# The w3 pieces of the experts issued by GpSimd from a queue of its own

## The chip, the cores and the metric

The kernel runs on one core of a Trainium2 chip. The time is device microseconds of one execution: 1745.23 us, the median of three runs (1743.76 to 1749.59).

## What is computed

Two layers of a backbone over 256 context and 256 latent tokens of width 1024. Each layer mixes tokens and then channels. The channel mixer of the second layer, on the latent tokens alone, is a mixture of 8 SwiGLU experts with hidden width 3584, two chosen for each token. It is the stage that the change touches. All weights are float32.

```python
def swiglu(h, w1, w3, w2):
    return (jax.nn.silu(h @ w1) * (h @ w3)) @ w2

def moe_swiglu(h, w_r, w1e, w3e, w2e):
    logits = (h @ w_r).astype(jnp.float32)
    vals, idx = lax.top_k(logits, TOP_K)
    wts = jax.nn.softmax(vals, axis=-1)
    comb = jnp.sum(jax.nn.one_hot(idx, N_EXPERTS, dtype=jnp.float32) * wts[..., None], axis=-2).astype(h.dtype)
    out = jnp.zeros_like(h)
    for e in range(N_EXPERTS):
        out = out + comb[..., e:e + 1] * swiglu(h, w1e[e], w3e[e], w2e[e])
    return out
```

## The kernel before

Each engine runs a program of its own, and semaphores tie them together. SyncE issues nearly all loads. First it loads the weights of both mixers and of the dense layer in chunks into the four slots of `ring` (loop from line 727, which waits for TensorE's last use of the slot). Then it loads the weights of the experts.

**Pieces.** An expert has 42 pieces of 1 MiB (`PIECE` = 2048 float32 on each of 128 partitions): 14 of w1, 14 of w3 and 14 of w2. A w1 or w3 piece is a block of rows and columns, 4 KiB per row in spans 0 to 2 and 2 KiB in the last; a w2 piece has 8 KiB on each partition. `ORDER` is the order of the pieces of an expert, in which they are loaded and used: for each span `s` of two blocks of 512 hidden columns, the pieces `("gu", s, i)`, where an even `i` is w1 and an odd `i` is w3, and then the `("dn", b, i)` pieces of w2 for the span before. In runs that is 8 gate and up pieces, 8 more, 4 of w2, 8, 4 of w2, 4, 4 of w2, 2 of w2.

**Slots.** There are 13 slots (`ESLOTS`): 12 in `ring` and one in `mixT`. Piece number n of all 336 goes to slot n mod 13 (`piece`). Before it is issued, its slot must be free: in the first turn when the last chunk that lay there was used (two piece slots for each chunk slot), and later when the piece 13 before it was used (`wait_free`, on a semaphore that TensorE raises). It raises `piece_in[s]` by 16 on landing, and `wait_piece` waits for 16 for each turn of that slot. SyncE issues all pieces, in the order of use, one after the other, lines 757 to 782: w1 and w3 at line 778, w2 at line 782. From the second expert on it reads the expert's number from `queue_i`, after one wait for `order_ready`.

**Use.** The experts are put in an order by their number of tokens. An expert with 65 to 128 tokens takes the path `mid`: ScalarE rounds each piece into one of three spare buffers (`HIGHS`, line 1849), VectorE takes the remainder in place (line 1962), and TensorE makes three products (lines 1361, 1363 and 1369). An expert with at most 64 tokens takes the path `few`: TensorE reads the piece itself, a w1 and a w3 piece in turn as a pair (line 1269), and w2 pieces at line 1309. Behind each expert come sums into the output (`add_slots`, line 1240) and the gathering of the next expert's tokens (line 1215).

**GpSimd** writes some index tables at the start (from line 792), and after a wait three more and the zeros of `yacc` (lines 799 to 802). Then its program is over.

Of the kernel before, what the change touches and what calls it, by code (L numbers as in the profile page):

```python
# [28 lines left out]
P = 128  # L29
# [292 lines left out]
def hybrid_backbone(nc, x, c, ctx_in, c_ctx, w_mod, b_mod, g_mix_pre, g_mix_post, w_in, w_decay, b_decay, gla_norm,  # L322
# [35 lines left out]
    with ExitStack() as stack:  # L358
# [3 lines left out]
        def sem(name):  # L362
            return stack.enter_context(nc.semaphore(name))
# [174 lines left out]
        piece_in = [sem(f"piece_in{i}") for i in range(ESLOTS)]  # L538
        piece_free = [sem(f"piece_free{i}") for i in range(ESLOTS)]
# [130 lines left out]

        def wait_piece(eng, e, key):
            s, turn_ = piece(e, key)
            eng.wait_ge(piece_in[s], 16 * (turn_ + 1))
# [48 lines left out]

        @block.sync
        def _(sp):
# [32 lines left out]
            for e in range(NE):  # L757
                expert = slice(0, 1)
                if e:
                    sp.wait_ge(order_ready, 1)  # L760
                    expert = bass.ds(sp.value_load(queue_i[0:1, 1, e:e + 1], min_val=0, max_val=NE - 1), 1)
                for key in ORDER:
                    s, turn_ = piece(e, key)
                    if turn_ == 0 and s < 2 * SLOTS:
                        sp.wait_ge(tile_ready, chunk_last[last_chunk[s // 2]] + 1)
                    elif turn_ == 0:

                        wait_tile(sp, ("mcol", 1, 11) if s == ESLOTS - 2 else ("y", 1, KD - 1))
                    else:
                        wait_free(sp, e * PER + PLACE[key] - ESLOTS)  # L770
                    dst = piece_words(e, key)
                    kind, n, i = key
                    if kind == "gu":
                        tiles = 4 // len(SPANS[n])
                        width = PIECE // tiles
                        w = e_w3 if i % 2 else e_w1
                        src = expert_rows(w, expert, (i // 2) * tiles * P, tiles, 2 * BLK * n, width)
                        sp.dma_start(dst.rearrange("p (k n) -> p k n", k=tiles), src).then_inc(piece_in[s], 16)  # L778
                    else:
                        r0 = n * BLK + i * 2 * P  # L780
                        src = e_w2[0, expert, r0:r0 + 2 * P, :].rearrange("e (p k) n -> p (e k n)", k=2)
                        sp.dma_start(dst, src).then_inc(piece_in[s], 16)  # L782
# [1896 lines left out]
```

## Time and profile before

| | us |
|---|---|
| median of three runs | 1745.23 |
| the profiled execution | 1745.67 |
| its span, first to last instruction | 1743.9 |
| TensorE busy | 1637.7 |
| VectorE busy | 955.5 |
| ScalarE busy | 537.0 |
| GpSimd busy | 4.1 |

The profiled execution moved 476.30 MB, 273 GB/s over its span. The experts' 336 pieces are 352.3 MB of that, in the last 900 us. An engine's busy time says how long its instructions ran, not that it was the limit; where the DMA engines are busy throughout and TensorE waits for a landing, the transfers are. The time to landing is measured from the issue and includes what stands ahead on the queue.

### The profile page before, as it was taken

Reading aid. Unit: us, or ns where it says so; the run is one execution under the profiler, and the core shown is the slowest. Engines: PE = TensorE matmul, PEld = TensorE weight load, DVE = VectorE, ACT = ScalarE, POOL = GpSimd, SP = SyncE. Lnnn points to the kernel's source line nnn. Section 1 sums busy time; section 2 is a strip of 40 time slices with the busy share of each in tenths; the row PEclk is TensorE's granted clock in tenths of the full one; section 3 lists DMA queues with packets and bytes.
Section 4 is the critical chain, followed back from the end, with each engine's and each line's share of the span. In section 5 each row is a group of like instructions: output and inputs, shape, how many; then the busy total and the mean of one; then the engine's idle time right before and its main releaser. Section 6 shows DMA issues by size and latency. Waiting matters only on the chain.

```text
span 1743.9 us, 21267 instructions
## 1 busy us (share of the span) xinstructions
PE 1637.7 (94%) x8432; PEld 1124.9 (65%) x8432; DVE 955.5 (55%) x1343; ACT 537.0 (31%) x682; POOL 4.1 (0%) x13
## 2 busy tenths in 40 slices
PE   6999999999999999998999999999989999887886
PEld 3788666788888885797788833887338873333322
DVE  4588765544445776699598712986129951111102
ACT  4421243400000005414577501774027730000001
POOL 0000000000000000000000000000000000000000
PEclk9999999999999999999999999999999999999998
DMA  9320785333321316327599999999999999999996
GB/s 357 138 97 1 278 302 185 105 97 97 97 97 37 133 64 229 110 85 290 225 380 373 348 390 408 412 408 411 414 407 412 409 407 406 408 412 409 410 415 264
DMA packets 160622, 476.30 MB, mean 273 GB/s; under 512 B 10002, under 2 KB 33012, under 8 KB 146164
## 3 DMA queue, kind: packets, MB, share of 16 engines
q1 hardware_dynamic: 158688, 474.24, 71.0%
q8 instruction: 78, 1.28, 0.3%
q10 hardware_dynamic: 1812, 0.41, 0.1%
q14 instruction: 44, 0.36, 0.1%
HBM read 473.58 MB, written 1.05 MB: 272 GB/s over the span
## 4 chain that ended last, share of the span: by engine, by line
PE 71%; SPq 13%; DMA 6%; DVE 4%; issue 3%; ACT 3%; ACTq 0%; DVEq 0%
PE ps L911 10%; PE ps L912 10%; PE ps L913 10%; SPq L778 10%; PE ps L1369 7%; PE ps L1361 6%; PE ps L1363 6%; PE ps L1269 6%; DMA ring<-in_e_w 4%; SPq L782 2%; PE ps L1309 2%; PE ps L875 2%; DMA ring<-in_w_mod 2%; PE ps L834 2%; PE ps L1215 1%
## 5 line engine op out<-in xcount | busy, mean ns | idle before, releaser
L1269 PE MATMUL ps<-ring,work 128*64 128x512 f32 x1040 | 256.0, 606 | 37.4 <-DMA ring<-in_e_w 30.3
L2518 DVE TENSOR_TENSOR norms<-work,ps 64x256 f32<-64x256 f32 x70 | 29.7, 424 | 327.4 <-ACT work L1828 325.8
L1269 PEld LDWEIGHTS ps<-ring,work 128*64 128x64 f32 x1040 | 83.5, 139 | 183.0 <-issue 180.6
L911 PE MATMUL ps<-ring_rounded 128*128 128x512 f32 (+1 forms) x536 | 190.5, 355 | 2.9 <-DVE norms L2300 1.6
L1962 DVE TENSOR_TENSOR ring_rounded<-ring,hT_rounded 128x2048 fp32r<-128x2048 f32 x77 | 174.3, 2286 | 18.5 <-ACT hT_rounded L1849 18.5
L913 PE MATMUL ps<-ring_rounded 128*128 128x512 f32 (+1 forms) x472 | 163.2, 346 | 0.0
L1849 ACT CAST hT_rounded<-ring 128x2048 fp32r<-128x2048 f32 x77 | 146.4, 1916 | 33.1 <-PE ps L1363 19.1
L913 PE MATMUL ps<-mixT_rounded,ring_rounded 128*128 128x512 f32 x328 | 127.6, 389 | 0.0
L1309 PE MATMUL ps<-ring,mixT 128*64 128x512 f32 x520 | 118.1, 596 | 4.9 <-DMA ring<-in_e_w 4.8
L911 PE MATMUL ps<-mixT_rounded,work_rounded 128*128 128x512 f32 x304 | 118.3, 389 | 0.0
L912 PE MATMUL ps<-hT_rounded,work_rounded 128*128 128x512 f32 x304 | 118.3, 389 | 0.0
L911 PEld LDWEIGHTS ps<-ring_rounded 128*128 128x128 f32 x536 | 101.3, 189 | 19.4 <-issue 2.3
L1959 DVE CAST work_rounded<-ring 128x1024 fp32r<-128x1024 f32 (+1 forms) x63 | 37.7, 599 | 113.2 <-PE ps L913 113.2
L1962 DVE TENSOR_TENSOR ring_rounded<-ring,ring_rounded 128x1024 fp32r<-128x1024 f32 (+1 forms) x89 | 97.1, 1092 | 3.8 <-ACT ring_rounded L1629 1.7
L913 PEld LDWEIGHTS ps<-ring_rounded 128*128 128x128 f32 x472 | 89.3, 189 | 11.1
L1962 DVE TENSOR_TENSOR ring_rounded<-ring,norms_rounded 128x2048 fp32r<-128x2048 f32 x39 | 89.2, 2288 | 11.7 <-ACT norms_rounded L1849 11.7
L912 PE MATMUL ps<-hT_rounded,ring_rounded 128*128 128x512 f32 (+1 forms) x280 | 95.4, 341 | 0.0
L1309 PEld LDWEIGHTS ps<-ring,mixT 128*64 128x64 f32 x520 | 36.8, 137 | 78.0 <-issue 65.6
L1361 PE MATMUL ps<-hT_rounded,work_rounded 128*128 128x512 f32 x216 | 85.2, 394 | 0.0
L1363 PE MATMUL ps<-hT_rounded,work_rounded 128*128 128x512 f32 x216 | 84.2, 390 | 0.0
L1369 PE MATMUL ps<-ring_rounded,work_rounded 128*128 128x512 f32 x308 | 82.9, 391 | 0.5 <-DVE ring_rounded L1962 0.4
L1849 ACT CAST norms_rounded<-ring 128x2048 fp32r<-128x2048 f32 x39 | 74.7, 1916 | 13.6 <-PE ps L1363 10.1
(295 smaller groups left out, 2714.0 us busy)
## 6 DMA issues: line engine op xcount, KB each, us to landing
ring<-in_e_w SPq DMA_DIRECT2D x311, 1024.0 KB, 18.3
ring<-in_w_mod SPq DMA_DIRECT2D x24, 2048.0 KB, 11.2
mixT<-in_e_w SPq DMA_DIRECT2D x25, 1024.0 KB, 18.4
ring<-in_w_in SPq DMA_DIRECT2D x12, 2048.0 KB, 8.7
ring<-in_w SPq DMA_DIRECT2D x22, 1024.0 KB, 8.1
ring<-in_w_out SPq DMA_DIRECT2D x4, 2048.0 KB, 15.5
ring<-in_w SPq DMA_DIRECT2D x4, 2048.0 KB, 7.7
ring<-in_w SPq DMA_DIRECT2D x2, 1536.0 KB, 9.7
```

The lines of the kernel that those rows point to most:

```text
L778: sp.dma_start(dst.rearrange("p (k n) -> p k n", k=tiles), src).then_inc(piece_in[s], 16)
L911: pe.matmul(acc, w_high_, x_high_, start=first, stop=False)
L912: pe.matmul(acc, w_high_, x_low_, start=False, stop=False)
L913: return pe.matmul(acc, w_low_, x_high_, start=False, stop=last)
L1269: ins = pe.matmul(narrow_bank(b)[H * w:H * w + H, :], xsel[:, k, 0:H], piece_words(e, pair[w])[:, at_:at_ + BLK], start=(k == 0), stop=(k ...
L1309: ins = pe.matmul(ps[0][H * half:H * half + H, :], eh[:, b % 2, ((j % 2) * 2 + j // 2) * H:][:, 0:H], piece_words(e, key)[:, o:o + BLK], s ...
L1361: pe.matmul(outs[q], high[q], w_high_[:, cols], start=q < first, stop=False, skip_group_check=True)
L1363: ins = pe.matmul(outs[q], low[q], w_high_[:, cols], start=False, stop=False, skip_group_check=True)
L1369: ins = pe.matmul(outs[q], high[q], w_low_[:, q * BLK:(q + 1) * BLK], start=False, stop=q >= 4 - last, skip_group_check=True)
L1849: act.copy(highs[at_ % HIGHS], piece_words(e, ORDER[n])).then_inc(high_ready, 1)
L1959: return dve.tensor_copy(dst, src)
L1962: return dve.tensor_tensor(dst, src, high, ALU.subtract)
```

## The change

The loop over experts and pieces becomes a function, `read_experts(eng, mine)`, which both SyncE and GpSimd run, each for its own pieces. `is_soft` picks the w3 pieces, and GpSimd issues them, behind the tables that it wrote before; its transfers run on a queue of its own. SyncE issues w1 and w2, in the same order as before with the w3 pieces left out. Slots, waits for free slots and `ORDER` stay. A w3 piece raises `piece_soft[s]` instead of `piece_in[s]`, and `wait_piece` waits for as many landings as its own semaphore has had for that slot. Both engines read the expert's number from `queue_i`.

```diff
+        piece_soft = [sem(f"piece_soft{i}") for i in range(ESLOTS)]
...
+        def is_soft(key):
+            return key[0] == "gu" and key[2] % 2 == 1
+
+        def landed(key):
+            return piece_soft if is_soft(key) else piece_in
+
+        landings = {}
+        for e_ in range(NE):
+            for key_ in ORDER:
+                s_ = piece(e_, key_)[0]
+                earlier = [n for of, at_, n in landings.values() if of is landed(key_) and at_ == s_]
+                landings[e_, key_] = (landed(key_), s_, len(earlier) + 1)
+
         def wait_piece(eng, e, key):
-            s, turn_ = piece(e, key)
-            eng.wait_ge(piece_in[s], 16 * (turn_ + 1))
+            of, s, n = landings[e, key]
+            eng.wait_ge(of[s], 16 * n)
...
+        def read_experts(eng, mine):
+
+            for e in range(NE):
+                expert = slice(0, 1)
+                if e:
+                    eng.wait_ge(order_ready, 1)
+                    expert = bass.ds(eng.value_load(queue_i[0:1, 1, e:e + 1], min_val=0, max_val=NE - 1), 1)
+                for key in [key for key in ORDER if mine(key)]:
+                    s, turn_ = piece(e, key)
+                    if turn_ == 0 and s < 2 * SLOTS:
+                        eng.wait_ge(tile_ready, chunk_last[last_chunk[s // 2]] + 1)
+                    elif turn_ == 0:
+
+                        wait_tile(eng, ("mcol", 1, 11) if s == ESLOTS - 2 else ("y", 1, KD - 1))
+                    else:
+                        wait_free(eng, e * PER + PLACE[key] - ESLOTS)
...
+                        eng.dma_start(dst.rearrange("p (k n) -> p k n", k=tiles), src).then_inc(landed(key)[s], 16)
...
+                        eng.dma_start(dst, src).then_inc(landed(key)[s], 16)
...
-            for e in range(NE):
...
+            read_experts(sp, lambda key: not is_soft(key))
...
             pool.memset(yacc, 0.0).then_inc(sums_clear, 1)
+            read_experts(pool, is_soft)
```

## Rows read from the trace of the kernel before

**Rows 1.** The page: 40 equal slices of the span, DMA busy tenths and moved GB/s.
```profile
DMA  9320785333321316327599999999999999999996
GB/s 357 138 97 1 278 302 185 105 97 97 97 97 37 133 64 229 110 85 290 225 380 373 348 390 408 412 408 411 414 407 412 409 407 406 408 412 409 410 415 264
```
**Rows 2.** Stretches of the expert stage, busy us and count of each engine.
```profile
core 0: us, PE busy (x) PEld busy (x) DVE busy (x) ACT busy (x) POOL busy (x), PEclk, DMA share, GB/s
1000.00:1727.00 727.00, 673.04 (x3064) 364.06 (x3060) 281.23 (x271) 209.72 (x195) 0.00 (x0) 0.99 1.02 407
...
1000.00:1090.00 90.00, 86.62 (x405) 33.26 (x402) 17.53 (x33) 11.29 (x20) 0.00 (x0) 1.00 1.00 396
1090.00:1210.00 120.00, 119.90 (x556) 99.85 (x555) 105.33 (x66) 82.58 (x55) 0.00 (x0) 1.00 1.02 411
1210.00:1307.00 97.00, 91.01 (x415) 35.39 (x413) 18.04 (x34) 12.23 (x20) 0.00 (x0) 0.98 1.02 410
1307.00:1427.00 120.00, 119.93 (x559) 100.25 (x558) 104.84 (x66) 82.27 (x55) 0.00 (x0) 1.00 1.02 411
1427.00:1530.00 103.00, 94.50 (x419) 36.62 (x419) 16.39 (x33) 7.86 (x17) 0.00 (x0) 0.97 1.02 406
1530.00:1630.00 100.00, 83.79 (x394) 31.80 (x392) 13.16 (x28) 7.38 (x16) 0.00 (x0) 1.00 1.02 411
```
**Rows 3.** First wide expert: its stretch, DMA issues with us to landing, TensorE's first product.
```profile
880.00:990.00 110.00, 110.00 (x506) 91.36 (x505) 97.16 (x59) 79.89 (x54) 0.00 (x0) 1.00 0.98 366
...
ring<-in_e_w SPq DMA_DIRECT2D x36, 1024.0 KB, 5.3
...
876.44 0.48 PE L1361 MATMUL ps<-hT_rounded,work_rounded 128*128 128x512 f32 x1
```
**Rows 4.** The chain that ended last, 1700 to 1744 us: start us, us, what.
```profile
1706.47 21.18 DMA ring<-in_e_w
1727.69 1.96 PE ps L1309 x8
```
**Rows 5.** DMA issues 1500 to 1700 us, median us from issue to landing.
```profile
ring<-in_e_w SPq DMA_DIRECT2D x69, 1024.0 KB, 19.0
```
**Rows 6.** SyncE's issues: all at line 778 (ns min/median/max), then 1523 to 1546 us.
```profile
L778 SPq DMA_DIRECT2D ring<-in_e_w x207: 367/777/12165, 846.3 to 1698.9; - x104
...
1523.55 14.53 SPq L778 DMA_DIRECT2D ring<-in_e_w  x5
1538.17 7.09 SPq L782 DMA_DIRECT2D ring<-in_e_w  x4
```
**Rows 7.** Waits of SyncE, 1190 to 1210 us: total, times, longest.
```profile
SPq L778 <- PE ps L1369: 18.0, 7, 3.9
```
**Rows 8.** DMA issues to landing at 1190:1210, 1210:1230 and 1427:1450 us.
```profile
ring<-in_e_w SPq DMA_DIRECT2D x7, 1024.0 KB, 14.4
...
ring<-in_e_w SPq DMA_DIRECT2D x7, 1024.0 KB, 12.2
...
ring<-in_e_w SPq DMA_DIRECT2D x8, 1024.0 KB, 9.7
```
**Rows 9.** Stretches at the second such boundary, and 1427:1450 in 40 slices.
```profile
1400.00:1427.00 27.00, 27.00 (x143) 23.08 (x141) 19.77 (x16) 13.78 (x11) 0.00 (x0) 1.00 1.02 409
1427.00:1450.00 23.00, 20.62 (x85) 7.95 (x85) 3.90 (x8) 1.66 (x3) 0.00 (x0) 1.00 1.00 388
...
GB/s 385 435 399 406 427 385 442 378 399 413 349 349 378 420 413 385 313 399 413 413 406 349 306 406 413 427 413 392 463 406 420 306 271 306 271 370 413 413 413 456
```
**Rows 10.** GpSimd in the whole span: busy us, mean ns; and its stretch.
```profile
L802 POOL MEMSET work<- 128x2048 f32 x1 | 1.8, 1822 | 0.0
...
800.00:850.00 50.00, 45.21 (x480) 38.85 (x483) 34.80 (x90) 26.68 (x51) 2.50 (x4) 1.00 0.52 189
```
**Rows 11.** VectorE by shape, 1090 to 1210 us: count, busy us, mean ns.
```profile
L1962 DVE TENSOR_TENSOR ring_rounded<-ring,hT_rounded 128x2048 fp32r<-128x2048 f32 x26 | 58.9, 2287 | 6.0 <-ACT hT_rounded L1849 6.0
```

More of the change, by code:

```diff
@@ L720, in count_of @@
             return eng.value_load(queue_i[0:1, 0, e:e + 1], min_val=0, max_val=SEQ)
+        def read_experts(eng, mine):
[12 more added lines that the diff above has]
+                        wait_free(eng, e * PER + PLACE[key] - ESLOTS)
+                    dst = piece_words(e, key)
+                    kind, n, i = key
+                    if kind == "gu":
+                        tiles = 4 // len(SPANS[n])
+                        width = PIECE // tiles
+                        w = e_w3 if i % 2 else e_w1
+                        src = expert_rows(w, expert, (i // 2) * tiles * P, tiles, 2 * BLK * n, width)
+                        eng.dma_start(dst.rearrange("p (k n) -> p k n", k=tiles), src).then_inc(landed(key)[s], 16)
+                    else:
+                        r0 = n * BLK + i * 2 * P
+                        src = e_w2[0, expert, r0:r0 + 2 * P, :].rearrange("e (p k) n -> p (e k n)", k=2)
+                        eng.dma_start(dst, src).then_inc(landed(key)[s], 16)
         @block.sync
@@ L755, in _ @@
                     sp.dma_start(d3[:, 0:nk], src).then_inc(full, 16)
-            for e in range(NE):
[L758 to L782, printed above, removed]
+            read_experts(sp, lambda key: not is_soft(key))
             for i in range(4):
```

## The prediction

> **What bounds the kernel now.** I read the slices of the page first, to find where the transfers are the limit. From the twenty-first slice (872 us) on, the DMA engines are busy nearly throughout, and from the twenty-fifth (1046 us) the moved rate stands near 410 GB/s [rows 1]. That is the stage that the change touches: 8 experts of 42 pieces of 1 MiB, 352.3 MB. The table of stretches then tells the experts apart [rows 2]. Where VectorE is busy for 105 of 120 us, an expert has 65 to 128 tokens and TensorE uses three products for each weight (I call it wide). Where VectorE is busy for under 20 us, an expert has at most 64 tokens (narrow). The order is wide, narrow, wide, narrow, wide and then three narrow. The first wide expert, about 876 to 999 us, has TensorE busy for 110 of 110 us at 366 GB/s [rows 3]: TensorE is the limit there. All that follows, 1000 to 1727 us, runs at 396 to 411 GB/s, in wide and narrow experts alike [rows 2], so the transfers are the limit. A piece costs 1.0486 MB / 0.410 MB per us = 2.56 us. The chain of waits agrees: its last transfer ends at 1727.7 us, and only 16.2 us of the 1743.9 us span follow [rows 4].
>
> The question is whether the DMA engines ever run out of issued pieces. Time from issue to landing, divided by 2.56 us, is the number in flight. In the three last narrow experts it is 19.0 us, 7.4 pieces [rows 5], and SyncE waits for no free slot: its issues follow each other without a gap, five in 14.5 us and then four in 7.1 us [rows 6]. So the queue itself is full, and of 13 slots about 3 stand empty (7.4 in flight, 2 or 3 landed and in use). At the end of a wide expert it is otherwise. There SyncE waits 18.0 of 20 us for TensorE to free slots [rows 7], and the landing time falls to 14.4 us, 5.6 pieces, and behind the boundary to 12.2 us, 4.8 pieces, and at the other such boundary to 9.7 us, 3.8 pieces [rows 8]. At that last one the rate is already down to 388 GB/s, with single slices of 0.6 us at 271 to 313 [rows 9]. In the first wide expert 5.3 us, 2.1 pieces, goes with 366 GB/s [rows 3]. I conclude that full rate wants about 2.5 pieces in flight at least; that number is an estimate between those two.
>
> **The change, part by part.**
> Removed from SyncE: 112 of 336 issues. An issue takes 0.37 us at the least [rows 6] and a piece takes 2.56 us, so SyncE had time for them. Its issues are long only because the queue is full. Worth: 0.
>
> Added on GpSimd: 112 issues, each behind a wait for its slot, and a register load for each expert. GpSimd has nothing else to do there: 0.00 us of work from 1000 us on [rows 2], and what stands ahead of the new loop on its queue, four instructions of 2.50 us in all, is done by 850 us [rows 10]. What is queued behind a waiting issue is only the next w3 piece. No issue from GpSimd stands in the trace. Lower bound: SyncE's 0.37 us. The nearest row above is GpSimd's memset over 128x2048, 1.8 us [rows 10]. The cost is nothing up to 3 x 2.56 = 7.67 us for each w3 piece (one piece in three). I take 2 us, the memset's, hidden by the pieces already in flight: 0 on the sum. If the cover were gone, each microsecond above 7.67 would cost 98 us (14 w3 pieces in each of the 7 experts after the first).
>
> Start: the first w3 piece waits for the same released slot as the first w1 piece (one chunk makes two slots), and the loads run from the first issue at 846.3 us [rows 6] to TensorE's first use at 876.4 us [rows 3], 30 us that routing fills. Worth: 0. The end: the last six pieces are w2, from SyncE, with GpSimd's queue empty by then, so the 16.2 us of tail [rows 4] stay.
>
> Landing semaphores: TensorE and ScalarE wait for the same pieces under other numbers, as many waits as before. Worth: 0.
>
> What is really moved is the order of landing. Before, pieces land in the order in which TensorE takes them. After, two queues feed the same 16 engines, and a w3 piece goes out as soon as its slot is free, past the w1 and w2 pieces that stand ahead of it on the other queue. Only a third of the pieces are w3 but their queue may take up to half of the rate, so GpSimd's queue runs ahead until slots stop it. A window of 13 pieces of `ORDER` holds 2 to 6 of w3 (few beside a run of w2 pieces, 6 in gates and ups alone), 13 x 14 / 42 = 4.3 on average; one of them is the partner that TensorE is about to use. So 1 to 5 pieces lie landed and unused while TensorE waits for a w1 or w2 piece. I take the average, 3.3. The bytes moved are the same and the engines stay busy, so in narrow experts that costs nothing: 3 slots stood empty there anyway. But TensorE is then those pieces behind, and a wide expert, 120 us of TensorE against 42 x 2.56 = 107.5 us of transfers, adds another 5 pieces. Those 5 had room before: 5.6 in flight was left. Now 3.3 slots fewer are left to be in flight. At the boundary with 4.8 in flight, 1.5 remain, 1.0 short of 2.5: 1.0 x 2.56 = 2.6 us of transfers not made. At the one with 3.8, 0.5 remain, 2.0 short: 5.1 us. Sum +7.7 us. With 1 piece ahead nothing is short, 0 us; with 5 it is 2.7 + 3.7 pieces, 16.4 us. The first wide expert starts with all slots full and is bound by TensorE, so I leave it out of the sum.
>
> The rate itself: one queue gave between 406 and 415 GB/s in the whole slices from 1046 to 1700 us [rows 1]. The engines are at 102% busy shares [rows 2], so there is no gap for a second queue to fill. I take no change. The bounds: from 1000 to 1727 us 727 us x 407 GB/s = 296 MB are moved [rows 2]. At 415, the best slice, that is 8.7 us less than at 410; at 396, the worst stretch behind 1000 us, it is 25.5 us more. The value is near 410 because all stretches of 1090 us and later but two read 410 or 411.
>
> On that one queue at 102% busy bears a rule of the Trainium skill, DMA: Bandwidth & Descriptors (section Issuing engines are not separate DMA queues): transfers from several engines interleave on the same 16 DMA engines, and only issuing time is saved. By it the sum of the change would be 0 plus the slot loss. The same page's section on bandwidth gives 425 GB/s for a 16 MB transfer issued from GpSimd; if that held for the whole mix, an estimate from that page is 296 / 0.425 = 696 us for the stage instead of 722 at 410, 26 us less. No row here shows such a rate.
>
> The span was 1743.9 us and the profiled execution 1745.67 us, 0.4 us over the median of the three runs, 1745.23. 1745.67 + 7.7 = 1753.4, less 0.4 gives 1753.0 us.
>
> **The rivals.**
> (a) Nothing that can be measured: the w3 pieces run ahead by 2 or fewer because GpSimd's issues come late or its queue holds few, and the rate stays (2 ahead: 0 + 0.8 pieces, 2 us). For it: 3 empty slots, full shares. It gives +0 to +4 us, 1745 to 1749; I put 1746.
> (b) Faster: two queues fed at once keep the engines better supplied. It needs time lost between packets, and the busy share of 102% speaks against it; the slices of 412 to 415 speak for a little of it. At 415 for the whole stage: 1745.2 - 8.7 = 1736.5 us, with no slot loss.
> (c) Slower by far: GpSimd cannot issue a w3 piece in 7.67 us. Then its queue sets the pace. At 9 us for one it is 98 x 1.33 = 130 us, 1875 us; at 8 us, 32 us, 1778 us. The decisive point is 7.67 us. Against it: 1.8 us for its memset over 128x2048, and nothing else on it.
> (d) GpSimd is held up by VectorE in wide experts. VectorE is busy for 105.33 of 120 us there, most of it by two-input TENSOR_TENSOR of 2.29 us (42 pieces; the largest group of them is 26, 58.9 us) [rows 11]. If those kept GpSimd from issuing, it would have the 120 - 105.33 = 14.7 us for 14 pieces, 1.05 us each; at 2 us for one, 13.3 us more in each of the three wide experts, so 40 us, 1785 us; the decisive point is 1.05 us of GpSimd's work for a piece.
> The trace has no GpSimd operation in those stretches. The Trainium skill, SBUF — State Buffer (section Who interferes with whom), has this rule: VectorE and GpSimd share a port pair with an exclusive lock, so descriptors written by GpSimd wait behind VectorE's copies in two-port modes, while a TENSOR_TENSOR takes only the read side. By it (d) would stay small.
> (e) The change doesn't do what it says: GpSimd's issues end in SyncE's queue and order. I see nothing for that; it is (a) in time.
>
> **How the numbers follow.** About 0.3%, 5 us, is what a measurement here can tell from no change: 1740 to 1750.5. Forecast 0.43 (of it 0.06 below 1750.5, with a small run-ahead), (a) with (e) 0.26, (b) 0.16, (c) 0.08, (d) 0.07. So faster 0.16, same 0.32, slower 0.52. The forecast's own range is 1745 to 1762 from the run-ahead, and with the rate's ends -8.7 and +25.5 on the forecast it is 1744 to 1779. The range for 8 in 10 takes in (b) and (d) as priced: 1733 to 1785. Outside are most of (c) and what lies beyond the rate's bounds.
>
> **What would show it.** In the changed kernel a new queue should carry 117 MB (112 pieces) and GpSimd's issues should stand beside SyncE's. Right: the landing time of w3 pieces well under that of w1 and w2 in narrow experts; TensorE waiting for w1 and w2 and hardly for w3; rates under 400 GB/s at 1190 to 1230 and 1400 to 1450 us, where it was 410, 388 and 409; rates of 410 elsewhere. The step on the rate is wrong if a narrow stretch like 1530 to 1630 moves off 411 by more than 5. Rival (c) would show as GpSimd's queue never waiting for slots and TensorE waiting for w3. Rival (d) would show as VectorE or GpSimd stretched in wide experts alone. If the last transfer still ends near 1727.7 with both boundaries at full rate, the run-ahead is the step that failed.

## The result and the profile after

The changed kernel takes 1762.15 us, the median of four runs (1760.57 to 1763.3), beside 1745.65 us for the kernel before on the same chip. The ratio is 1.0094, with a 95% interval of 1.0082 to 1.0106: it is slower by 16.5 us, where 7.7 were forecast. The profiled execution took 1761.06 us with a span of 1759.4 us, 15.5 more than the 1743.9 of before.

Of the page of the changed kernel: moved rate in 40 slices of the span, the DMA queues (packets, MB, share of 16 engines), VectorE's largest product and GpSimd's issues (busy us, mean ns of one | idle before them), and the time to landing.

```profile
GB/s 357 134 96 1 293 282 207 80 97 98 100 99 43 116 120 171 144 57 280 286 364 377 346 410 407 412 411 378 409 408 412 411 348 382 408 412 409 410 413 243
...
q1 hardware_dynamic: 124128, 356.80, 53.5%
q0 software_dynamic: 30464, 117.45, 17.1%
...
L1982 DVE TENSOR_TENSOR ring_rounded<-ring,hT_rounded 128x2048 fp32r<-128x2048 f32 x77 | 174.3, 2285 | 18.0 <-ACT hT_rounded L1869 18.0
...
L760 POOL DMA_DIRECT2D ring<-in_e_w x104 | 75.3, 724 | 740.6 <-PE ps L1389 288.2
...
ring<-in_e_w SPq DMA_DIRECT2D x207, 1024.0 KB, 18.6
ring<-in_e_w POOLq DMA_DIRECT2D x104, 1024.0 KB, 12.4
```

The new queue carries 117.45 MB, the w3 pieces, so the change does what it says. An issue on GpSimd takes 0.72 us and GpSimd waits for slots most of the time. VectorE's product takes 2285 ns, 2287 in [rows 11]. Against [rows 1], two stretches have lost rate: the twenty-eighth slice (378, was 411) and the thirty-third and thirty-fourth (348 and 382, were 407 and 406). Those are the ends of the second and the third wide expert.

The stretches of [rows 2] in the changed kernel, with the two boundaries by themselves (1200 to 1230 and 1420 to 1460 us):

```profile
core 0: us, PE busy (x) PEld busy (x) DVE busy (x) ACT busy (x) POOL busy (x), PEclk, DMA share, GB/s
...
1090.00:1210.00 120.00, 118.15 (x548) 97.33 (x545) 104.65 (x65) 86.88 (x58) 10.13 (x14) 1.00 1.02 408
1210.00:1307.00 97.00, 91.64 (x416) 36.86 (x414) 18.16 (x34) 7.28 (x16) 10.13 (x14) 0.96 1.01 397
1200.00:1230.00 30.00, 30.00 (x137) 19.55 (x138) 15.87 (x16) 7.29 (x6) 3.58 (x5) 1.00 0.98 364
1307.00:1427.00 120.00, 117.64 (x544) 95.99 (x543) 103.15 (x64) 84.53 (x57) 9.39 (x13) 1.00 1.02 408
1420.00:1460.00 40.00, 36.48 (x156) 22.43 (x156) 15.35 (x15) 7.30 (x6) 3.58 (x5) 0.96 0.88 311
1427.00:1530.00 103.00, 92.81 (x413) 39.94 (x413) 19.94 (x34) 9.44 (x18) 10.12 (x14) 0.95 0.96 373
1530.00:1630.00 100.00, 83.83 (x376) 31.02 (x374) 12.90 (x27) 7.00 (x15) 9.40 (x13) 0.97 1.02 410
```

The same two boundaries of the kernel before:

```profile
1200.00:1230.00 30.00, 30.00 (x137) 16.08 (x137) 10.87 (x14) 4.32 (x6) 0.00 (x0) 1.00 1.03 411
1420.00:1460.00 40.00, 37.62 (x168) 17.49 (x169) 10.09 (x19) 2.89 (x6) 0.00 (x0) 1.00 1.01 399
```

At the first boundary (411 - 364) x 30 us = 1.4 MB is not moved, 1.3 pieces, 3.4 us. At the second it is (399 - 311) x 40 = 3.5 MB, 3.4 pieces, 8.6 us. That makes 12.0 us. Elsewhere the rate stands: 408 in the wide experts, 410 in the narrow one. So the bytes are lost at two places of some 35 us and nowhere else. TensorE's clock is not the reason: it was granted 1.00 in the wide experts and at the first boundary of both kernels. At the second it is 0.96, where it was 1.00, but so it is in the kernel below with all pieces on GpSimd, which takes 1748.54 us.

Where TensorE stands when they are lost is told by the first high product of each wide expert (count: ns min/median/max, first and last start). It started at 1088.5 and 1305.0 us in the kernel before; in the changed one:

```profile
L1381 PE MATMUL ps<-hT_rounded,work_rounded x72: 387/389/475, 1096.4 to 1193.7; 128*128 128x512 f32 x72
...
L1381 PE MATMUL ps<-hT_rounded,work_rounded x72: 387/389/475, 1315.3 to 1412.9; 128*128 128x512 f32 x72
```

From 846 to 1200 us both kernels moved 389 GB/s, so up to there the bytes are equal. TensorE is 7.9 us behind with the same bytes, so bytes of 7.9 / 2.56 = 3.1 pieces have been moved ahead of their turn, in landed pieces and in parts of others. At the second it is 10.3 us behind, of which 3.4 are bytes lost at the first boundary: 6.9 us, 2.7 pieces.

The issue and landing times of the single pieces show what that lead is. At the first high product the first w1 and the first w3 piece of the expert have landed in the kernel before, and nothing behind them. In the changed kernel two more w3 pieces have, past a w1 piece that is still missing, in both wide experts. At the end of the wide experts hardly a piece lies past a missing one any more (0.02 and 0.06 on the mean at 1200 to 1230 and 1420 to 1460 us); what is left of the lead is that TensorE is late, and pieces that landed in order wait for it in their slots. Counted in the same way, 2.7 and 2.2 pieces are in flight at the two boundaries, where the kernel before has 5.0 and 4.4.

One sign of the prediction did not come: "TensorE waiting for w1 and w2 and hardly for w3". Who waited for the w3 pieces (us, times):

```profile
  PE ps L1289: 20.4, 5
```

Four of the five waits, 3.4 to 6.1 us each, are for the last w3 piece of a narrow expert, which comes late; in two of them a w2 piece behind it in the order has landed first. The fifth is 0.9 us. So both kinds of disorder stand in the changed kernel: w3 pieces that are early at the start of an expert, and one that is late at its end.

The rest is at the end. The chain that ended last in the changed kernel (start us, us, what):

```profile
1716.20 12.22 DMA ring<-in_e_w
1728.42 0.14 issue
1728.56 5.25 PE ps L1289 x16
1733.80 5.15 PE ps L1329 x24
1738.95 0.43 PE ps L1316 x2
1739.39 5.33 PE ps L1329 x24
```

GpSimd's last issue in the timeline, with the idle time before it in brackets:

```profile
1716.20 0.75 POOL L760 DMA_DIRECT2D ring<-in_e_w  x1 [12.89 <-issue]
```

And the last stretches, in the columns of the table above:

```profile
1735.00:1740.00 5.00, 5.00 (x26) 1.80 (x24) 0.41 (x1) 0.37 (x1) 0.00 (x0) 1.00 0.72 301
1740.00:1745.00 5.00, 4.69 (x22) 1.29 (x18) 0.20 (x1) 0.21 (x1) 0.00 (x0) 1.00 0.01 5
```

Nearly all bytes are there by 1740 us. The last two pieces, w2, were issued at 1716.8 and 1717.3 us:

```profile
DMA to landing us min/median/max: 21.8/22.8/23.8
```

So the last landed at 1741.1 us, 13.4 us later than in [rows 4], near the 12.0 above. But the transfer that TensorE waits for is a w3 piece of the last span, landed at 1728.4, and all the last span's work, 16 us, stands behind it; before, 1.96 us of TensorE's work followed the last landing. From the last landing to the end of the span it is 18.3 us now, and was 16.2. That adds 2.1 us: 13.4 + 2.1 = 15.5, the whole difference of the spans. GpSimd issued this piece after 12.89 us of idle time that ends in nothing the profile shows. Such idle times are 187 us of GpSimd's program, in 23 places. Of the eleven long ones, 10 to 14 us, eight stand at w3 pieces of the last span, whose runs are of 2 KiB where others have 4.

### The profile page after: what moved, and what is told of

Same layout as the page of the kernel before. It is cut to its first block, busy times and chain, and to the rows that moved or that the text cites. A ratio compares the mean times of both kernels' runs of the same rounds, so it can differ in the third digit from the quotient of the medians.

```text
span 1759.4 us, 21388 instructions
## 1 busy us (share of the span) xinstructions
PE 1647.1 (94%) x8432; PEld 1125.4 (64%) x8432; DVE 955.5 (54%) x1343; ACT 536.2 (30%) x682; POOL 85.1 (5%) x125
## 3 DMA queue, kind: packets, MB, share of 16 engines
q0 software_dynamic: 30464, 117.45, 17.1%
## 4 chain that ended last, share of the span: by engine, by line
PE 76%; DMA 11%; issue 5%; DVE 5%; ACT 2%; SPq 1%; ACTq 0%; DVEq 0%; POOL 0%; POOLq 0%
PE ps L931 10%; PE ps L933 10%; PE ps L932 10%; PE ps L1289 10%; PE ps L1389 7%; PE ps L1381 6%; PE ps L1383 6%; DMA ring<-in_e_w 6%; PE ps L1329 3%; DMA mixT<-in_e_w 3%; PE ps L895 2%; PE ps L854 2%; SPq L764 1%; PE ps L1260 1%; PE ps L1235 1%
## 5 line engine op out<-in xcount | busy, mean ns | idle before, releaser
L1289 PE MATMUL ps<-ring,work 128*64 128x512 f32 x1040 | 266.5, 625 | 36.7 <-DMA ring<-in_e_w 17.7
L1982 DVE TENSOR_TENSOR ring_rounded<-ring,hT_rounded 128x2048 fp32r<-128x2048 f32 x77 | 174.3, 2285 | 18.0 <-ACT hT_rounded L1869 18.0
L1869 ACT CAST hT_rounded<-ring 128x2048 fp32r<-128x2048 f32 x77 | 146.3, 1916 | 31.6 <-PE ps L1383 18.4
L1329 PE MATMUL ps<-ring,mixT 128*64 128x512 f32 x520 | 118.1, 596 | 11.7 <-DMA ring<-in_e_w 11.6
L760 POOL DMA_DIRECT2D ring<-in_e_w x104 | 75.3, 724 | 740.6 <-PE ps L1389 288.2
L1982 DVE TENSOR_TENSOR ring_rounded<-ring,norms_rounded 128x2048 fp32r<-128x2048 f32 x39 | 89.2, 2287 | 12.2 <-ACT norms_rounded L1869 12.2
## 6 DMA issues: line engine op xcount, KB each, us to landing
ring<-in_w_out SPq DMA_DIRECT2D x4, 2048.0 KB, 15.5
```

Of the source, the lines that this page charges most:

```text
L760: eng.dma_start(dst.rearrange("p (k n) -> p k n", k=tiles), src).then_inc(landed(key)[s], 16)
L1289: ins = pe.matmul(narrow_bank(b)[H * w:H * w + H, :], xsel[:, k, 0:H], piece_words(e, pair[w])[:, at_:at_ + BLK], start=(k == 0), stop=(k ...
L1329: ins = pe.matmul(ps[0][H * half:H * half + H, :], eh[:, b % 2, ((j % 2) * 2 + j // 2) * H:][:, 0:H], piece_words(e, key)[:, o:o + BLK], s ...
L1869: act.copy(highs[at_ % HIGHS], piece_words(e, ORDER[n])).then_inc(high_ready, 1)
L1982: return dve.tensor_tensor(dst, src, high, ALU.subtract)
```

## The experiments

The theory after the result was the prediction's: two queues change the order of landing, w3 pieces fill slots ahead of their use, and the slots are missing at the ends of wide experts. The rivals were GpSimd's late pieces (too little room for their descriptors in `dynamic_dma_scratch_size`, 1024 bytes), and two queues on the same engines as such. Unless it is said otherwise, edits are to the changed kernel. All give the reference's computation in full.

**Room for GpSimd's descriptors.**

```diff
-dynamic_dma_scratch_size=1024)
+dynamic_dma_scratch_size=4096)
```

> The changed kernel with GpSimd's descriptor scratch at 4096 bytes per partition instead of 1024, all else the same. Two theories for the 16.5 us that the change costs. Run-ahead (of the prediction): w3 pieces land early and take slots. A larger scratch then changes nothing or lets them run further ahead: 1760 to 1768 us, the stretch 1427:1530 again near 373 GB/s. Store (new): GpSimd's queue can hold few descriptors, the w3 pieces of the last span (512 runs of 2 KiB, twice as many as the others) wait 10 to 14 us for room and land late, TensorE waits for them and starts each wide expert 8 to 10 us later with as many bytes landed, so the slots fill at its end. Then a larger scratch takes away most of the cost: 1745 to 1750 us, GpSimd's idle time that ends in nothing visible (186 us in the changed kernel) under 60 us, wide experts starting within 3 us of before (1088.5 and 1305.0 us).

Measured: 1764.61 us, ratio to before 1.0101 (1.0084 to 1.0118). The cause is not the lack of room, in this version. GpSimd's idle time that ends in nothing visible fell from 187 us to 12.6 us, its own line being:

```profile
  issue: 12.6, 2
```

So the waits were for room, and they are gone. TensorE's waits for w3 pieces are gone too:

```profile
  PE ps L1289: 0.8, 1
```

But the w3 pieces only ran further ahead: three more of them, not two, have landed at the first high product, and TensorE now waits for w2 pieces, 37.4 us in 26 times, where it was 11.6 in 9. That product starts at 1098.7 and 1322.4 us, later than in the change, and the rates at the two boundaries are 341 and 323 GB/s. The end of the span is as far behind the last landing as in the change, 18.4 us.

**The w3 pieces of the last span back to SyncE.**

```diff
-            return key[0] == "gu" and key[2] % 2 == 1
+            return key[0] == "gu" and key[2] % 2 == 1 and key[1] < NS - 1
```

> The changed kernel with the two w3 pieces of the last span of each expert (16 of 112) issued by SyncE again, scratch 1024 as in the changed kernel. Store theory: those pieces are the ones with 512 runs; without them GpSimd's queue never waits 10 to 14 us for room, only the short waits of 4 to 5 us stay: 1746 to 1752 us. Run-ahead theory: 96 of 112 pieces still run ahead, 1757 to 1764 us, both boundaries at reduced rate.

Measured: 1762.08 us, 1.0093 (1.0076 to 1.0109); the first product of the wide expert at 1097.3 us, 345 and 313 GB/s at the boundaries. Alone it gives nothing. The end of the span is 16.4 us behind the last landing again, so those 2 us were due to the last span; the transfers end later for it.

**A w3 piece is issued only when the piece five places before it has landed.**

```diff
+                    at_ = e * PER + PLACE[key]
+                    if is_soft(key) and at_ >= 5:
+                        wait_piece(eng, (at_ - 5) // PER, ORDER[(at_ - 5) % PER])
```

> The changed kernel, scratch 1024, with one more wait: GpSimd issues a w3 piece only when the piece 5 places before it in the order of use has landed, so it can be at most 5 places ahead. Run-ahead theory: the lead is gone, 1745 to 1752 us. Store theory: what costs time is that w3 pieces come late, and a wait more can only make them later: 1762 to 1790 us.

Measured: 1764.46 us, 1.0099 (1.0082 to 1.0116). Alone it gives nothing either: 1098.7 and 1321.1 us, 326 and 319 GB/s. (Its profiled execution was the slowest of four, 1769.46 us.) Now TensorE waits for w3 pieces far more:

```profile
  PE ps L1292: 56.6, 18
```

Taken by itself this spoke against the run-ahead, and it stayed open until both edits were made together.

**All pieces on GpSimd, in the old order, with the room of the first experiment.** One queue again, but GpSimd's.

```diff
-            return key[0] == "gu" and key[2] % 2 == 1
+            return True
...
-dynamic_dma_scratch_size=1024)
+dynamic_dma_scratch_size=4096)
```

> GpSimd issues all 336 pieces, w1, w2 and w3, in the order of use, scratch 4096 bytes; SyncE issues none of them. One queue again, so nothing can pass anything. It prices GpSimd's queue alone. If its descriptors cost no rate: 1744 to 1750 us and 408 to 412 GB/s in the narrow experts. If transfers from GpSimd are slower by themselves (rate under 405 in the stretch 1530:1630), more than 1755 us. Run-ahead theory: 1745, since order is kept. Store theory: 1745 to 1750, as about 12 pieces of 17 entries fit in four times the room.

Measured: 1748.54 us, 1.0013 (1.0004 to 1.0023). An issue takes GpSimd 0.72 us for a w1 or w3 piece and 0.54 us for a w2 piece, and the wide experts start at 1087.6 and 1304.0 us. The two boundaries:

```profile
1200.00:1230.00 30.00, 30.00 (x137) 15.73 (x137) 11.22 (x16) 3.48 (x5) 7.86 (x12) 1.00 1.03 409
1420.00:1460.00 40.00, 37.56 (x160) 17.19 (x160) 9.14 (x19) 2.89 (x6) 9.47 (x15) 0.96 0.97 378
```

The second boundary is under the 399 of before, which goes with the 0.13%. So neither GpSimd's issues nor its transfers are what costs the 16.5 us. What remains is the order, or the two queues.

**Every second piece on GpSimd.** Two queues with half of the pieces each.

```diff
-            return key[0] == "gu" and key[2] % 2 == 1
+            return PLACE[key] % 2 == 1
```

> GpSimd issues every second piece in the order of use (all w3 pieces, and the second piece of each pair of w2), SyncE the others, scratch 1024. Both queues then carry the same run sizes in the same order, half of the pieces each. Packet theory (new, from the changed kernel's packets: between 1072 and 1085 us the two queues moved 492 packets each but 3.49 and 1.89 MB; the engines take a packet of each queue in turn, so the shares go by packet size and not by need, pieces land out of order, and TensorE waits for one piece while bytes of later ones land): in even queues the order is nearly kept, 1745 to 1751 us, wide experts starting within 3 us of before. Two queues as such (a loss for each switch between a hardware and a software queue): as slow as the change or slower, 1760 to 1770 us, since more packets come from GpSimd.

Measured: 1768.77 us, 1.0141 (1.0117 to 1.0165), where 1745 to 1751 were expected: a miss. That half and half would keep step was wrong. The wide experts start at 1097.2 and 1320.4 us. With the room of 4096 bytes as well:

> The even split of run e5 (every second piece from GpSimd) with the scratch at 4096 bytes. In e5 GpSimd's queue waited 385 us in all for room (its idle time that ends in nothing visible), 11 us ahead of each piece of the last span, and SyncE's pieces passed them: that was the disorder there. Packet theory: with room for them both queues go in step and order is nearly kept: 1745 to 1751 us. Two queues as such: 1760 us or more again.

Measured: 1768.91 us, 1.0136 (1.012 to 1.0153), the same miss, so it isn't the room. The DMA queues of this last kernel at 1540 to 1570, 1572 to 1580 and 1610 to 1620 us:

```profile
q0 software_dynamic: 1464, 6.57, 54.1%
q1 hardware_dynamic: 1461, 5.73, 47.9%
...
q1 hardware_dynamic: 346, 1.96, 59.7%
q0 software_dynamic: 346, 1.34, 41.8%
...
q0 software_dynamic: 493, 3.15, 77.3%
q1 hardware_dynamic: 489, 0.97, 26.1%
```

The two queues move packets one for one (1464 and 1461, 346 and 346, 493 and 489), and packets are not equal in size. In the first and the third GpSimd's queue moves more, in the second less. The third is the last span of an expert: there SyncE's w1 pieces go in packets of 2 KiB (0.97 MB in 489), while GpSimd's pieces have 4 KiB and more. That is where step is lost: in the second expert every GpSimd piece lands behind the SyncE piece before it in the order down to place 33 (of 42, counted from 0), and the w3 piece at place 35 lands 5.8 us ahead of the w1 piece at place 34. Equal numbers of pieces don't keep two queues in step. No kernel with equal packets in both queues was run.

**The last span on SyncE and the throttle, together.**

```diff
-            return key[0] == "gu" and key[2] % 2 == 1
+            return key[0] == "gu" and key[2] % 2 == 1 and key[1] < NS - 1
...
+                    at_ = e * PER + PLACE[key]
+                    if is_soft(key) and at_ >= 5:
+                        wait_piece(eng, (at_ - 5) // PER, ORDER[(at_ - 5) % PER])
```

> The two edits of the second and third run together: w3 of the last span issued by SyncE, and GpSimd's w3 pieces issued only when the piece 5 places before has landed. Alone, neither gave anything back (1762.1 and 1764.5 us). Packet theory: the throttle stops the lead of the 4 KiB pieces, and the 2 KiB pieces of the last span can no longer be pushed back behind the 8 KiB pieces of w2 in the other queue; each edit alone leaves the other disorder. Together 1746 to 1754 us. Two queues as such: 1758 to 1765 us.

Measured: 1747.7 us, 1.0012 (1.0001 to 1.0023). Nearly all of the 16.5 us are back, with two queues and a w3 queue of its own for three spans of four. The line of the first high product, in both wide experts:

```profile
L1384 PE MATMUL ps<-hT_rounded,work_rounded x72: 387/389/475, 1088.6 to 1185.5; 128*128 128x512 f32 x72
...
L1384 PE MATMUL ps<-hT_rounded,work_rounded x72: 387/389/475, 1304.7 to 1402.4; 128*128 128x512 f32 x72
```

The two boundaries:

```profile
1200.00:1230.00 30.00, 30.00 (x138) 16.03 (x138) 11.24 (x15) 4.04 (x5) 2.87 (x4) 1.00 1.03 410
1420.00:1460.00 40.00, 37.63 (x170) 17.65 (x170) 10.27 (x19) 2.89 (x6) 3.59 (x5) 1.00 0.99 387
```

And GpSimd's issue at the end of a narrow expert in the timeline:

```profile
1072.93 0.72 POOL L763 DMA_DIRECT2D ring<-in_e_w  x1 [38.36 <-DMA ring<-in_e_w]
```

The starts are those of the kernel before within 0.3 us, and the first boundary runs at its rate. GpSimd is held for 38 us on a landing, while SyncE's pieces pass alone; it no longer takes slots for the next expert.

**The same with a distance of nine places instead of five.**

```diff
-                    if is_soft(key) and at_ >= 5:
-                        wait_piece(eng, (at_ - 5) // PER, ORDER[(at_ - 5) % PER])
+                    if is_soft(key) and at_ >= 9:
+                        wait_piece(eng, (at_ - 9) // PER, ORDER[(at_ - 9) % PER])
```

> Run e6 (last span's w3 on SyncE, throttle) with the distance at 9 in place of 5: a w3 piece may be issued up to 9 places ahead of what has landed. At 5 it was 1747.7 us, without a limit (slots give 12) 1762.1 us. If the cost grows with how far pieces pass each other: 1750 to 1757 us, the wide experts starting 2 to 5 us late. If the wait of itself did something else (fewer packets in flight, slower pace of GpSimd): 1746 to 1749 us again.

Measured: 1756.3 us, 1.0058 (1.0041 to 1.0075). More freedom to run ahead, more time: starts at 1096.8 and 1315.5 us, 352 and 337 GB/s. With the distance alone changed, the time moves by 8.6 us (8.0 by the ratios), so the distance is what counts.

**The w2 pieces on GpSimd instead of w3.** They stand in runs of four and two, so a queue of them can run ahead further.

```diff
-            return key[0] == "gu" and key[2] % 2 == 1
+            return key[0] == "dn"
```

> GpSimd issues the w2 pieces (8 KiB runs, 112 of them) in place of the w3 pieces; SyncE issues w1 and w3; scratch 1024. Packet theory: beside 4 KiB and 2 KiB pieces, w2 takes two thirds and four fifths of the rate and lands as early as slots let it, up to six pieces in a run, while gates and ups wait: more disorder than in the change, 1762 to 1785 us, narrow experts with TensorE waiting for w1 and w3 alone. Two queues as such: 1757 to 1762 us, as fewer packets come from GpSimd.

Measured: 1791.15 us, 1.0263 (1.0246 to 1.0281), above the upper end of the expectation by 6 us. The starts are 1104.0 and 1332.2 us, 15.5 and 27.2 us behind the kernel before, about twice the delay of the change, and more than twice. (Its profiled execution, 1784.0 us, was the fastest of four, so the delays of the others are larger.) TensorE waits for w1 and w3 alone, as expected.

**Every second piece on GpSimd, with the throttle and the room.** It asks whether the two queues cost anything once order is kept.

```diff
-            return key[0] == "gu" and key[2] % 2 == 1
+            return PLACE[key] % 2 == 1
...
+                    at_ = e * PER + PLACE[key]
+                    if is_soft(key) and at_ >= 5:
+                        wait_piece(eng, (at_ - 5) // PER, ORDER[(at_ - 5) % PER])
...
-dynamic_dma_scratch_size=1024)
+dynamic_dma_scratch_size=4096)
```

> The even split of run e8 (every second piece from GpSimd, scratch 4096) with the throttle: GpSimd issues a piece only when the piece 5 places before it has landed. e8 took 1768.9 us though both queues have the same pieces to move. Packet theory: nothing holds the queues in step there; the one that reaches the 8 KiB pieces of w2 first gets twice the bytes for each turn and draws ahead. With the lead cut to 5 places order comes back: 1747 to 1754 us, wide experts starting within 4 us of before. Two queues as such: 1764 us or more, as half of the packets still come from GpSimd.

Measured: 1748.88 us, 1.0024 (1.0014 to 1.0034). The throttle alone takes 20 of the 24 us from the version without it. The boundaries run at 411 and 385 GB/s, the wide experts start at 1088.5 and 1304.8 us. Two queues as such cost no more than 0.24% (0.34 by the interval).

**The throttle with the room, w3 pieces of all spans on GpSimd.** It asks what kept the throttle alone from helping.

```diff
+                    at_ = e * PER + PLACE[key]
+                    if is_soft(key) and at_ >= 5:
+                        wait_piece(eng, (at_ - 5) // PER, ORDER[(at_ - 5) % PER])
...
-dynamic_dma_scratch_size=1024)
+dynamic_dma_scratch_size=4096)
```

> Run e3 (all w3 from GpSimd, throttle at 5 places) with the scratch at 4096 bytes. e3 took 1764.5 us, and the same throttle with the last span's w3 on SyncE 1747.7 us (e6). If what was left in e3 is the wait for room in front of the last span's pieces (GpSimd idle for 9.7 us at 1050 to 1060 us with nothing visible ending it): 1747 to 1753 us now. If it is their place in the packets' turns, one third of the rate beside the 8 KiB pieces of w2 that should come after them: 1756 to 1765 us still.

Measured: 1751.05 us, 1.0031 (1.0017 to 1.0045). With the throttle, room is worth 12 to 13 us (1764.46 to 1751.05, or 0.68% by the ratios); without it, room was worth nothing (1762.15 and 1764.61). TensorE's waits for w3 pieces are half of those with the throttle alone:

```profile
  PE ps L1292: 27.8, 13
```

The two causes stand one behind the other: either disorder alone, w3 pieces early or w3 pieces late for lack of room, costs the full 16.5 us or more, and where the run-ahead is taken away the lateness is what is waited for. That is why neither edit alone showed anything. The boundaries (394 and 357 GB/s) are still under those of the version with the last span on SyncE; what makes up these last 3 us was not taken apart.

**What a slot is worth.** The kernel before and the changed kernel with 12 slots for 13:

```diff
-ESLOTS = RINGW // PIECE + 1
+ESLOTS = RINGW // PIECE
```

> The kernel before with 12 slots in place of 13 (ESLOTS), one queue in order. It prices a slot: 3.8 and 4.8 pieces in flight at the two boundaries become 2.8 and 3.8, against about 2.5 wanted for full rate: 1746 to 1752 us. If slots are not what limits there: 1745 to 1747 us.

> The changed kernel with 12 slots in place of 13. If its cost is that landed pieces which TensorE can't use yet fill the slots at the end of the wide experts, one slot less costs one piece more at each of the two boundaries, 2 x 2.56 us, and a little in the first wide expert: 1767 to 1773 us, 5 to 10 us over the change. If the cost is anywhere else (rate, issue, the last expert): 1762 to 1765 us.

Measured: 1750.96 us for the kernel before so edited, 1.0025 (1.0012 to 1.0038), 4.4 us more (2 to 7 by the interval). For the changed kernel it is 1766.35 us (1760.4 to 1768.1), 1.0114 (1.0088 to 1.0139), some 4 us over the change. That lies between the two expectations, and the intervals overlap: this run decides nothing, and that a slot is dearer after the change than before is not shown. The boundaries of the kernel before with 12 slots:

```profile
1200.00:1230.00 30.00, 30.00 (x137) 16.63 (x137) 10.63 (x13) 4.53 (x5) 0.00 (x0) 1.00 1.03 407
1420.00:1460.00 40.00, 37.45 (x161) 18.45 (x161) 11.73 (x20) 3.10 (x7) 0.00 (x0) 0.96 0.92 350
```

With one queue and nothing out of order, a missing slot shows where the change does, nearly all of it at the second boundary: (411 - 407) x 30 + (399 - 350) x 40 us are 2.1 MB, 5.1 us. Pieces in flight are 3.8 and 2.8, just one less.

The last column of the table below counts the pieces in flight (issued and not yet landed) on the mean of the same two stretches, from the single issue and landing times.

| kernel | us | first high product, 2nd and 3rd wide expert | GB/s at 1200:1230, 1420:1460 | in flight there |
|---|---|---|---|---|
| before | 1745.65 | 1088.5, 1305.0 | 411, 399 | 5.0, 4.4 |
| last span on SyncE, distance 5 | 1747.7 | 1088.6, 1304.7 | 410, 387 | 5.1, 4.1 |
| all on GpSimd, one queue | 1748.54 | 1087.6, 1304.0 | 409, 378 | 4.7, 3.6 |
| every second, distance 5, room | 1748.88 | 1088.5, 1304.8 | 411, 385 | 4.9, 3.9 |
| before, 12 slots | 1750.96 | 1089.5, 1306.6 | 407, 350 | 3.8, 2.8 |
| distance 5, room | 1751.05 | 1091.3, 1306.5 | 394, 357 | 3.6, 3.0 |
| last span on SyncE, distance 9 | 1756.3 | 1096.8, 1315.5 | 352, 337 | 2.9, 2.6 |
| last span on SyncE | 1762.08 | 1097.3, 1317.2 | 345, 313 | 2.3, 2.1 |
| the change | 1762.15 | 1096.4, 1315.3 | 364, 311 | 2.7, 2.2 |
| distance 5 | 1764.46 | 1098.7, 1321.1 | 326, 319 | 2.4, 2.7 |
| room | 1764.61 | 1098.7, 1322.4 | 341, 323 | 2.7, 2.1 |
| change, 12 slots | 1766.35 | 1099.6, 1321.4 | 325, 323 | 2.0, 1.9 |
| every second | 1768.77 | 1097.2, 1320.4 | 335, 313 | 2.8, 2.3 |
| every second, room | 1768.91 | 1096.3, 1315.5 | 362, 307 | 2.9, 2.3 |
| w2 on GpSimd | 1791.15 | 1104.0, 1332.2 | 348, 335 | 2.3, 2.4 |

Whatever starts the wide experts within 2 us of before stays within 0.25% of its time, and the more they are late, the slower it mostly is. The rate falls with the pieces in flight, whether one queue moves them or two: at the first boundary it is 394 GB/s and more with 3.6 or more, and 325 to 364 with 2.9 or fewer; at the second 350 and more with 2.8 or more, and 307 to 337 with 2.7 or fewer. No version is faster than the kernel before.

## Why the prediction was right in its direction and short in its size

**What bounds the kernel: right.** The transfers do, and bytes not moved are time: 12.0 us of them by the rates, 13.4 by the last landing.

**Issues, landing semaphores, start: right.** GpSimd's issue was put at 2 us and takes 0.72. The rivals (c), GpSimd sets the pace, and (d), VectorE holds it up, fall with it, though TensorE does wait for some w3 pieces: GpSimd waits for slots most of the time, issues take 702 to 836 ns over the whole stage, those in wide experts among them, and one engine issued all pieces in 1748.54 us. As to (d), the Trainium skill, SBUF — State Buffer (section Who interferes with whom), had VectorE's two-input products leave GpSimd's descriptors alone, and that agrees here.

**The rate: right.** 410 GB/s at 1530 to 1630 us, where 411 was read; it didn't move by 5. Rival (b), faster, falls with it.

**The run-ahead: near in size, wrong in its reason.** 3.3 pieces were taken; bytes of 3.1 and 2.7 pieces were found ahead of their turn, two whole w3 pieces among them. What is missing in flight is less, 2.3 and 2.2 pieces. Right was also that the boundaries fall under 400 GB/s; that TensorE would hardly wait for w3 was not. The time to landing is well shorter for w3 than for the others, as was said. The issues of 1540 to 1740 us, with the median time to landing:

```profile
ring<-in_e_w SPq DMA_DIRECT2D x45, 1024.0 KB, 25.5
ring<-in_e_w POOLq DMA_DIRECT2D x21, 1024.0 KB, 13.3
```

The reason given was that the queue "may take up to half of the rate". That holds only where packets are equal. The queues of the changed kernel at 850 to 870 us, w3 beside w1, and at 1064 to 1071 us, w3 beside w2:

```profile
q0 software_dynamic: 1081, 4.18, 51.9%
q1 hardware_dynamic: 1046, 4.03, 50.2%
...
q1 hardware_dynamic: 256, 1.85, 65.5%
q0 software_dynamic: 259, 1.00, 35.5%
```

Against w1, in 4 KiB packets as its own, the new queue has half; against w2, in 8 KiB, a third. The packets go one for one. The Trainium skill, DMA: Bandwidth & Descriptors (section Queues, rings and completion order), says that an engine takes its queues in turn by whole packets, and these rows agree as to the turns; whether its packet, of several descriptors, is the one of the profile no row here tells. My expectations for the kernels with every second piece had the rule but took the packets of both queues to be equal, and so missed by 18 us.

**The price of the missing slots: the step that failed.** The sum had 2.6 + 5.1 us at the two boundaries; measured are 3.4 and 8.6. It rested on "full rate wants about 2.5 pieces in flight at least", an estimate between two stretches. In the changed kernel the issues land after 7.1 to 7.5 us at 1200 to 1230 us, and with 364 GB/s this is 2.5 pieces in flight (2.7 by the count of single pieces):

```profile
ring<-in_e_w POOLq DMA_DIRECT2D x5, 1024.0 KB, 7.5
ring<-in_e_w SPq DMA_DIRECT2D x4, 1024.0 KB, 7.1
```

So 2.5 gives 364, not 410. By the prediction's rule the 2.7 and 2.2 pieces that were left would have cost nothing and 0.3 of a piece, 0.8 us in all; they cost 12.0. That the sum came to 7.7 is owed to a second error the other way: it had only 1.5 and 0.5 left. The kernel before with 12 slots says the same: it had 4.8 and 3.8 in flight by the prediction's reckoning, one less leaves 3.8 and 2.8, by its rule enough, at no cost; it cost 4.4 us. By the table, 5 pieces go with 411 GB/s and 3.8 with 407 at the first boundary; at the second, where the mean hides more, 4.4 go with 399, 3.6 with 378 and 2.8 with 350. So the rate begins to fall somewhere near 4 pieces, an estimate from these rows, and there is no one number for it.

The mean hides that TensorE frees slots in bursts, by my reading: at the boundary, where it sums and gathers, it frees none, and transfers nearly stop in single slices. In 40 slices of 1420 to 1450 us in the changed kernel:

```profile
GB/s 399 421 404 399 339 322 322 399 421 339 279 388 410 322 317 393 393 284 218 371 426 366 350 355 382 224 202 366 382 382 153 76 126 262 399 404 175 137 224 371
```

Slices of 76 to 153 GB/s stand where the slowest of [rows 9] was 271. SyncE waits for a wide expert's releases up to 6.7 us at a time (total, times, longest, 1175 to 1230 us), where the kernel before had 28.5 us in 12 waits and 3.9 for the longest; GpSimd now has waits of its own beside it:

```profile
SPq L760 <- PE ps L1389: 34.7, 7, 6.7
```

That the bursts make the loss, and how much of it, no run takes apart: how the rate falls with the pieces in flight is read off the table, and why stays open.

**The end: missed.** "The 16.2 us of tail stay" counted that the last six pieces come from SyncE. It didn't look at who is late: a w3 piece of the last span, issued at 1716.20, which landed before them but after its turn. The tail grew by 2.1 us, a term that the sum did not have, and it was 16.4 us again with the last span on SyncE. Together: 13.4 us by the last landing (12.0 by the rates) and 2.1, against 7.7.

The range up to 1785 held the time only through the room left for rivals and for the rate. The run-ahead's own far end, 1762 us, meets the measured time by luck: its condition was 5 pieces ahead (at the second boundary fewer than none in flight), and what happened was 3 ahead, at a higher price.

## What to carry to other kernels

Where loads feed a ring of slots in the order of use, splitting them over two queues gives that order up, and pieces that landed early occupy slots that the late ones need; it is paid where the fewest pieces are in flight, so look there first. If two queues are wanted, tie the second to the landings of the first (here a wait for the piece five places before gave back 14 of 16.5 us together with the last span on the old queue, and 20 of 24 us in another split), and see that its own pieces don't come late. A mean of pieces in flight underrated the need here, perhaps because slots come free in bursts: don't set a threshold between two stretches that differ in other ways, but price a slot by taking one away from the kernel before.

## What the runs showed of the hardware

- Two queues on the same DMA engines take packets one for one, so bytes are shared as the packet sizes: 1.85 to 1.00 MB at 256 and 259 packets.
- GpSimd's queue alone reaches the rate of SyncE's: 409 GB/s at 1200 to 1230 us with all pieces on it, 411 before. An issue of 1 MiB takes it 0.70 to 0.84 us for a w1 or w3 piece and 0.53 to 0.56 us for a w2 piece of 128 runs.
- Its packets are 4 KiB also for pieces whose runs are 2 KiB, and SyncE's are not: 30464 packets on its queue are 112 pieces of 272. Giving 16 pieces of the last span back to SyncE takes 4352 packets off its queue (272 each) and puts 8448 on SyncE's (528 each).
- With 1024 bytes for descriptors GpSimd stood idle for up to 14 us before an issue, most before pieces of 512 runs, with no releaser in the profile, 187 us in all; with 4096 bytes 12.6 us were left. In the change taking them away gained nothing; behind the throttle it gained 12 to 13 us.
- The rate of this stream of 1 MiB pieces falls with the pieces in flight: 411 GB/s with 5.0, 407 with 3.8, 364 with 2.7 at one boundary; 399 with 4.4, 350 with 2.8, 311 with 2.2 at the other.
